# A feed-forward block in split fp32: weight sums stored by the first pass and loaded by the second, and low parts made by VectorE

## The chip, the cores and the metric

One core of a Trainium2 chip runs the whole program in one launch. The metric is the device time of one execution in microseconds (us). Below, TensorE is PE in the rows, VectorE is DVE, ScalarE is ACT, GpSimd is POOL, and SyncE, which here only issues transfers, is SP.

## What is computed

One layer of a hybrid transformer, over a prompt of 2048 tokens and a sample of 32 tokens: projections, two kinds of attention, an output projection, and a feed-forward block. Only the last matters here:

```python
def conv_ffn(h, conv_state, w_up, w_conv, b_conv, w_down):
    u = h @ w_up                                   # 1024 -> 2 x 2816
    padded = jnp.concatenate([conv_state, u], axis=1)
    uc = sum(padded[:, j:j + T] * w_conv[j] for j in range(CONV_W)) + b_conv
    a, g = jnp.split(uc, 2, axis=-1)
    return (jax.nn.silu(a) * g) @ w_down, padded[:, -(CONV_W - 1):]
```

The rest of the program, ahead of the block, is the same in both kernels.

## The kernel before, in words

**Split fp32.** Every factor x of a product is held as a high part (a copy in the type fp32r, made by ScalarE) and a low part (x minus the high part, made by VectorE or GpSimd). A product of two such factors is three matmuls: high by high, high by low, low by high (`three`, L2416 to L2423).

**Two passes over the up weights.** `w_up` is taken in 22 pairs of 128-column tiles: tile F (the half that goes through silu) and tile G. The 2080 tokens are five blocks of WT = 416. The first pass (wide, pairs 0 to 21) makes three blocks for each pair, the second (narrow, pairs 22 to 43, the same 22 weight tiles again) makes two. Two blocks at a time go through a Strassen scheme of seven products of half the depth, P1 to P7, four steps of depth each; the wide pass makes its third block in the plain way (SF and SG, eight steps each). So PE issues 7 x 4 x 3 = 84 matmuls of 416 columns for a narrow pair and 84 + 48 = 132 for a wide one. Its order is written out: P1, P5, P6, P2, (SF), P7, P3, P4, (SG) (`wide_pair`, `narrow_pair`, L2480 to L2499).

**What a pair needs.** P1, P2 and SF read the halves of tile F (`fwH`, `fwL` in the rows), P4 the second half of G and SG all of it, and P5, P6, P7, P3 read four sums of halves of F and G. VectorE makes the sums from the loaded tiles `fraw` (`sum_one` to `sum_four`, L2060 to L2077; `fsum_plain`, `fsL_plain`), ScalarE their high parts (`high_sum`, `fsH`), GpSimd their low parts (`low_sum`, L1608 to L1611, `fsL`). GpSimd also makes the low parts of both tiles (`low_half`, L1603 to L1606, `fwL`) and of some blocks of h2 (`low_block`, L1613 to L1615, `fright`). Both passes make the same sums.

**The other work of a pair.** The Strassen scheme chains through PSUM: ScalarE copies bank a to bank b (`seed_b`) and b to c (`seed_c`) between products, and takes bank e (`take_e`). VectorE takes two results (`take_c22`, which P4 of the same pair waits for, L2475 to L2478; `take_c12`), runs the three taps of the convolution over `fV` for F and for G (`taps`, L2095 to L2109), and multiplies silu(F) by G (`product`, L2137 to L2140). SyncE then stores the product to `act_d`. VectorE's slot of pair g is in this order: convolution G of pair g-1, product g-1, sums one and two of pair g+1, take c22, sum three, take c12, sum four, convolution F of pair g (`wide_slot`, `narrow_slot`, L2142 to L2161).

**Between the passes** the right-hand blocks are replaced: SyncE loads `late_blocks`, B11 and B21 (L1546 to L1552), VectorE makes T1 to T4 from them, ScalarE the high parts, VectorE and GpSimd the low parts (L2306 to L2338).

**Behind the second pass** `down(n)` multiplies 17 activation tiles by rows of `w_down` (66 matmuls of 512 columns for each tile and half); the 22 rows' low parts are shared by GpSimd (BY_POOL, L1677 to L1681) and VectorE (BY_DVE, `first_low`).

**Queues.** SyncE's queue runs in the order that it is written in: a wait at its head holds every later load and store. Of the second pass it is

```python
def next_up(g, i):
    sp.wait_ge(w_low[F], g + 1)
    sp.wait_ge(sums_ready, 4 * g + 4)
    load_up(i, F)
    sp.wait_ge(w_low[G], g + 1)
    load_up(i, G)
...
with sp.Fori(1, NF - 1) as i:
    next_up(NF + i, i + 1)
    store_narrow(i - 1)
```

## Time and profile before

| | |
|---|---|
| time, median of 3 runs | 3193.68 us (3192.21 to 3194.82) |
| time of the profiled execution | 3200.23 us |
| its span, first to last instruction | 3198.5 us |
| PE busy | 3009.9 us, 94% |
| VectorE busy | 1958.1 us, 61% |
| ScalarE busy | 1306.1 us, 41% |
| GpSimd busy | 1120.1 us, 35% |
| feed-forward up part | about 1649 to 2654 us of the span |
| data moved | 359.19 MB, mean 112 GB/s |

The profiled execution took 6.5 us more than the median of the runs. Times in the rows below are microseconds from the start of its span. A matmul's own time (0.35 us for 416 columns) overlaps the next one's, so the pace of PE is the count of matmuls over a stretch, not their durations.

### The profile page before, as it was taken

The page shows a single profiled execution, that of the slowest core. Times are in us where ns is not written, and L with a number is a line of the kernel's source. Part 1 is how long each engine was busy: PE and PEld are TensorE (multiplying, and loading weights), DVE is VectorE, ACT ScalarE, POOL GpSimd, SP SyncE. Part 2 cuts the span into 40 slices and gives each one's busy share as a digit, 9 for nine tenths or more (in the row PEclk, how much of TensorE's full clock was granted, in tenths as well). Part 3 has the DMA queues.
Part 4 walks back from the last instruction along what each step waited for, and adds up shares of the span by engine and source line. Part 5 has one row for each costly group of instructions (what it writes and reads, how often), then busy time and mean ns, then how long its engine had stood idle before and what let it go on. Part 6 is the DMA issues. An engine that isn't in the chain of part 4 may idle for free.

```text
span 3198.5 us, 48166 instructions
## 1 busy us (share of the span) xinstructions
PE 3009.9 (94%) x17216; PEld 2605.0 (81%) x17216; DVE 1958.1 (61%) x2517; ACT 1306.1 (41%) x2452; POOL 1120.1 (35%) x892
## 2 busy tenths in 40 slices
PE   7999998998999998999999999998899998999998
PEld 5788887776777887888879999998788886887886
DVE  2300035522998998675678787777999996224221
ACT  4611122213777887344554444444333333113110
POOL 3311012212666676120135444445555552002000
PEclk8999999998999999899999999999999999999999
DMA  6312224424422430885642222223222235434332
GB/s 216 112 65 77 73 82 143 134 96 115 126 56 55 90 69 16 274 275 186 217 144 73 68 65 68 67 68 97 70 80 81 79 97 185 166 125 162 124 126 71
DMA packets 299510, 359.19 MB, mean 112 GB/s; under 512 B 66204, under 2 KB 218456, under 8 KB 292572
## 3 DMA queue, kind: packets, MB, share of 16 engines
q1 hardware_dynamic: 283166, 307.83, 31.5%
q0 software_dynamic: 14864, 49.31, 4.5%
q8 instruction: 95, 1.56, 0.2%
q14 instruction: 53, 0.43, 0.0%
q10 hardware_dynamic: 1332, 0.06, 0.0%
HBM read 248.23 MB, written 108.89 MB: 112 GB/s over the span
## 4 chain that ended last, share of the span: by engine, by line
PE 40%; DVE 10%; issue 7%; DMA 2%; DVEq 1%; ACT 1%; POOL 0%; SPq 0%; ACTq 0%; POOLq 0%
PE facc L2422 16%; PE dacc L2528 14%; PE eacc L2401 6%; DVE fV L2099 2%; DVE fsum_plain L2063 1%; DVE fU L2126 1%; DVE fsL_plain L2072 1%; PE mpT L2548 1%; DVE fV L2103 1%; PE mpm L2558 1%; DVE fV L2108 1%; PE mpD L2539 0%; DMA w_out_plain<-w_out 0%; PE eyT L2384 0%; PE mpS L2568 0%
## 5 line engine op out<-in xcount | busy, mean ns | idle before, releaser
L2528 PE MATMUL dacc<-drows,dact 128*128 128x512 f32 (+1 forms) x2200 | 516.5, 397 | 16.4 <-DVE drows L2167 5.4
L2528 PEld LDWEIGHTS dacc<-drows,dact 128*128 128x128 f32 (+1 forms) x2200 | 412.6, 188 | 119.8 <-DVE drows L2167 6.2
L716 PE MATMUL pacc<-pring,h1H 128*128 128x512 f32 x1360 | 436.5, 398 | 8.8 <-POOL pring L584 5.5
L2422 PE MATMUL facc<-fright,fsH 128*128 128x416 f32 x1408 | 385.8, 355 | 18.0 <-ACT facc L1750 9.0
L1090 POOL TENSOR_TENSOR aS<-aS,aC 128x512 f32<-128x512 f32 (+3 forms) x326 | 334.6, 1034 | 166.8 <-DVE aC L1050 157.4
L1050 DVE TENSOR_TENSOR_SCAN aC<-aB,aC,a 128x512 f32<-128x512 f32 (+3 forms) x326 | 362.8, 1113 | 21.9 <-ACT aB L1008 10.6
L1605 POOL TENSOR_TENSOR fwL<-fraw,fwH 128x1024 fp32r<-128x1024 f32 x88 | 206.5, 2348 | 424.8 <-ACT fwH L1750 424.5
L2422 PE MATMUL facc<-fright,fwH 128*128 128x416 f32 x1056 | 302.2, 369 | 53.9 <-DVE fU L2087 49.2
L716 PEld LDWEIGHTS pacc<-pring,h1H 128*128 128x128 f32 x1360 | 259.6, 191 | 63.7 <-POOL pring L584 6.6
L2422 PEld LDWEIGHTS facc<-fright,fsH 128*128 128x128 f32 x1408 | 265.9, 191 | 24.8 <-issue 13.0
L2422 PEld LDWEIGHTS facc<-fright,fwH 128*128 128x128 f32 x1056 | 207.0, 198 | 65.0 <-issue 56.2
L716 PE MATMUL pacc<-pring,h1L 128*128 128x512 f32 x640 | 250.5, 393 | 0.0
L2422 PE MATMUL facc<-fright,fsL 128*128 128x416 f32 x704 | 250.2, 355 | 0.0
L2173 DVE TENSOR_TENSOR dact<-dact_plain,dact 128x2816 fp32r<-128x2816 f32 (+1 forms) x34 | 100.6, 2962 | 219.6 <-ACT dact L1750 219.6
L1750 ACT ACTIVATE dact<-dact_plain 128x2816 fp32r<-128x2816 f32 (+1 forms) x34 | 83.4, 2452 | 368.3 <-DMA dact_plain<-act_d 368.3
L1106 PE MATMUL a_z<-ak,aq 128*128 128x512 f32 (+3 forms) x640 | 209.7, 411 | 15.1 <-DMA aq<-qk_T 15.1
L1008 ACT ACTIVATE aB<-a_z 128x512 f32<-128x512 f32 (+3 forms) x326 | 180.1, 553 | 45.9 <-PE a_z L1117 21.0
L1132 PE MATMUL a_x<-ident,aS 128*128 128x128 f32 x1106 | 182.8, 282 | 10.2 <-ACT aA L1017 8.4
L2422 PE MATMUL facc<-fright,fwL 128*128 128x416 f32 x528 | 192.3, 364 | 0.0
L324 ACT ACTIVATE pstage<-pacc 128x512 f32<-128x512 f32 x112 | 66.6, 595 | 303.4 <-PE pacc L716 303.3
L2422 PE MATMUL facc<-fh,fwH 128*128 128x416 f32 x704 | 189.9, 351 | 0.0
L1626 POOL DMA_DIRECT2D y_out<-dy x34 | 18.4, 541 | 483.4 <-DVE dy L2190 483.4
(319 smaller groups left out, 6033.7 us busy)
## 6 DMA issues: line engine op xcount, KB each, us to landing
fraw<-w_up SPq DMA_DIRECT2D x88, 512.0 KB, 3.9
dact_plain<-act_d SPq DMA_DIRECT2D x32, 1408.0 KB, 6.4
proj_out<-pstage SPq DMA_DIRECT2D x119, 256.0 KB, 2.0
qk_T<-pturn POOLq DMA_DIRECT2D x68, 256.0 KB, 3.0
mwa<-w_ada SPq DMA_DIRECT2D x16, 1024.0 KB, 5.7
praw<-w_in SPq DMA_DIRECT2D x56, 256.0 KB, 2.8
aq<-qk_T SPq DMA_DIRECT2D x28, 512.0 KB, 12.0
mx<-proj_out SPq DMA_DIRECT2D x51, 256.0 KB, 5.0
```

Of the source, the lines that this page charges most:

```text
L716: op = mm_(acc[:, n % NB], h[:, kk, tok(t)], weight(q, w), start=(j == 0), stop=(j == len(order) - 1))
L1008: nc.scalar.activation(part(B, RB, n), part(Z, NZ, n), ACT.Sigmoid, scale=-1.0).then_inc(pass_ready, 1)
L1050: v.tensor_tensor_scan(buf[:, a:b][:, ::-1], part(B, RB, n)[:, ::-1], nought[:, 0:width(n)], buf[:, b:b + 1], ALU.mult, ALU.add).then_inc( ...
L1090: nc.gpsimd.tensor_tensor(at, at, buf[:, a + 1:b + 1], ALU.mult).then_inc(w_ready, 1)
L1106: mm = nc.tensor.matmul(to, Q[:, b, half, i * P:(i + 1) * P], K[:, b, span], start=(half == 0), stop=(half == 1), skip_group_check=True)
L1132: mm = nc.tensor.transpose(X[:, n % NX, j * P:(j + 1) * P], src[:, j * P:(j + 1) * P], c["ident"][:])
L1605: nc.gpsimd.tensor_tensor(upL[:, j, cols], raw[:, j, cols], upH[:, j, cols].bitcast(F32), ALU.subtract).then_inc(w_low[j], 1)
L1750: copy = lambda to, at: nc.scalar.activation(to, at, ACT.Copy)
L2173: v.tensor_tensor(to, acts_plain[n % 3][:, 1, :, 0:w], at[:, 0, :, 0:w].bitcast(F32), ALU.subtract).then_inc(a_low, 1)
L2401: mm = nc.tensor.matmul(acc[:, 1 - i.u, cols], a[:, i.u, kk], w[:, kk, cols], start=(kk == 0 and n == 0), stop=(kk == KD - 1 and n == len( ...
L2422: mm = nc.tensor.matmul(bank, a[:, kk], b[:, kk], start=(begins and kk == 0 and m == 0), stop=(kk == count - 1 and m == 2), skip_group_che ...
L2528: mm = nc.tensor.matmul(down_acc[0:rows, n % 2], at[:, l, kk, 0:rows], r, start=(kk == 0 and m == 0), stop=(kk == NF - 1 and m == len(pass ...
```

## The change

The four sums of a pair, high and low, stand side by side in one tile `fsums`. The first pass stores each split sum to HBM (`sums_d`, 4 x 512 KB for a pair); the second pass loads them instead of making them, and so needs only the second half of tile G. VectorE makes the low parts of tile F, of the sums and of the blocks; GpSimd keeps the low part of tile G. VectorE makes the low parts of all 22 rows of `w_down`. Slots of ScalarE, VectorE and SyncE are put in another order, and ScalarE's table for silu is loaded once ahead of the first pass. PE's order of products is the same; P5, P6, P7 and P3 of the second pass wait for loads.

```diff
+            def load_second(g, i):
+                sp.wait_ge(w_low[G], g + 1)
+                sp.dma_start(raw[:, G, KH:KD], d["w_up"].rearrange("(q p) n -> p q n", p=P)
+                             [:, KH:KD, bass.ds(FF + i * P, P)]).then_inc(raw_in[G], 16)
+            def store_sums(i):
+                own = bass.ds(i, 1)
+                for n in range(4):
+                    sp.wait_ge(s_low, 4 * i + n + 1)
+                    sp.dma_start(d["sums_d"][own, n].rearrange("o p e -> p (o e)"),
+                                 sums[:, n].bitcast(F32).rearrange("p a k e -> p (a k e)")).then_inc(sums_stored, 16)
+            def load_sum(n, g, i):
+                sp.wait_ge(done[("P5", "P6", "P7", "P3")[n]], g)
+                own = bass.ds(i, 1)
+                sp.dma_start(sums[:, n].bitcast(F32).rearrange("p a k e -> p (a k e)"),
+                             d["sums_d"][own, n].rearrange("o p e -> p (o e)")).then_inc(sums_in[n // 2], 16)
...
+            def narrow_loads(i):
+                sp.wait_ge(w_low[F], NF + i + 1)
+                load_up(i + 1, F)
+                load_second(NF + i, i + 1)
                 store_narrow(i - 1)
+                for n in range(4):
+                    load_sum(n, NF + i + 1, i + 1)
+            with sp.Fori(1, NF - 3) as i:
+                narrow_loads(i)
...
             def high_sum(n, g):
+                if n == 0:
+                    at_least(act, sums_stored, 64 * g)
...
                 seed_c(g)
+                high_sum(0, g + 1)
+                high_sum(1, g + 1)
                 take_c11(g, 2 + WT)
                 take_sf(g)
                 high_half(F, g + 1)
-                for n in range(4):
-                    high_sum(n, g + 1)
+                high_sum(2, g + 1)
+                high_sum(3, g + 1)
...
-            low_block(B11, b_first[0], 1)
-            low_sum(0, 0)
-            low_sum(1, 0)
-            low_block(B21, b_first[1], 2)
             store_h2(final)
-            low_sum(2, 0)
-            low_block(B22, b_first[2], 3)
-            low_sum(3, 0)
             with pool.Fori(1, NF) as i:
-                prepare(i, False)
...
+                low_half(G, i)
+            with pool.Fori(0, NF) as i:
+                low_half(G, NF + i, slice(KH, KD))
...
                 product(g - 1, WIDE)
                 sum_one(g + 1)
                 sum_two(g + 1)
+                low_sum(0, g + 1)
+                low_sum(1, g + 1)
+                low_half(F, g + 1)
                 take_c22(g, 2 + 2 * WT)
                 sum_three(g + 1)
+                low_sum(2, g + 1)
                 take_c12(g, 2 + 2 * WT)
                 sum_four(g + 1)
+                low_sum(3, g + 1)
                 conv_wide(g, g, F)
 
             def narrow_slot(g, i):
                 conv_narrow(g - 1, i - 1, G)
                 product(g - 1, NARROW)
-                sum_one(g + 1)
-                sum_two(g + 1)
+                low_half(F, g + 1)
                 take_c22(g, 2 + WT, True)
-                sum_three(g + 1)
                 take_c12(g, 2 + WT, True)
-                sum_four(g + 1)
                 conv_narrow(g, i, F)
...
+            def sums_are_in(n, g, wide):
+                if wide:
+                    pe.wait_ge(s_low, 4 * g + n + 1)
+                else:
+                    pe.wait_ge(sums_in[n // 2], 32 * (g - NF + 1))
```

The instructions of VectorE in the loop over narrow pairs, from the product of pair g-1 to the taking of c12, before:

```order
L2140 TENSOR_TENSOR fV<-fV 128x832
L2061 ISA
L44 ISA
L2063 TENSOR_TENSOR fsum_plain<-fraw 128x512
L2066 REGISTER_ALU
L44 REGISTER_ALU
L2068 TENSOR_TENSOR fsum_plain<-fsum_plain,fraw 128x512
L2087 TENSOR_TENSOR fU<-facc,fE 128x384
L2087 TENSOR_TENSOR fU<-facc,fE 128x32
L2072 TENSOR_TENSOR fsL_plain<-fraw 128x512
L2093 TENSOR_TENSOR fU<-facc,fE 128x384
L2093 TENSOR_TENSOR fU<-facc,fE 128x32
```

and now:

```order
L2178 TENSOR_TENSOR fV<-fV 128x832
L2084 REGISTER_ALU
L2085 TENSOR_TENSOR fwL<-fraw,fwH 128x1024
L2122 REGISTER_ALU
L2125 TENSOR_TENSOR fU<-facc,fE 128x384
L2125 TENSOR_TENSOR fU<-facc,fE 128x32
L2131 TENSOR_TENSOR fU<-facc,fE 128x384
L2131 TENSOR_TENSOR fU<-facc,fE 128x32
```

The sums (the fourth stands behind these rows, L2077) are gone; the low part of tile F has come in, ahead of the taking of c22.

SyncE's queue in the same loop, before (ISA rows are waits and set-up of the next transfer):

```order
L1441 DMA fraw<-w_up 128x8x128
L1441 ISA
L1441 DMA fraw<-w_up 128x8x128
L1465 ISA
L1465 DMA act_d<-fV 128x32
L1466 ISA
L1466 DMA act_d<-fV 128x6x128
L1468 ISA
L1468 DMA act_d<-fV 128x32
```

and now, of one of the pairs that are written out behind the loop:

```order
L1439 DMA fraw<-w_up 128x8x128
L1451 DMA fraw<-w_up 128x4x128
L1481 DMA act_d<-fV 128x32
L1482 DMA act_d<-fV 128x6x128
L1484 DMA act_d<-fV 128x32
L1464 DMA fsums<-sums_d 128x1024 x4
```

The second load of weights is half as large, and four loads of sums stand behind the three stores of the product.

SyncE's queue between the passes, before (`flate_blocks` are the late blocks, `fright_plain` are B11 and then B21):

```order
L1546 DMA flate_blocks<-h_d 128x8x416
L1441 DMA fraw<-w_up 128x8x128 x2
L1455 DMA act_d<-fV 128x9x128
L1457 DMA act_d<-fV 128x96
L1550 DMA fright_plain<-h_d 128x4x416
L1552 DMA fright_plain<-h_d 128x4x416
```

and now:

```order
L1565 DMA flate_blocks<-h_d 128x8x416
L1439 DMA fraw<-w_up 128x8x128
L1451 DMA fraw<-w_up 128x4x128
L1571 DMA fright_plain<-h_d 128x4x416
L1464 DMA fsums<-sums_d 128x1024 x2
L1471 DMA act_d<-fV 128x9x128
L1473 DMA act_d<-fV 128x96
L1577 DMA fright_plain<-h_d 128x4x416
```

B11's load stands ahead of the store of the product of pair 20, for which it had waited.

## Rows read from the trace of the kernel before

**Rows 1.** Busy time by stretch: the wide pass, then the narrow.
```profile
core 0: us, PE busy (x) PEld busy (x) DVE busy (x) ACT busy (x) POOL busy (x), PEclk, DMA share, GB/s
1721.00:2196.00 475.00, 475.00 (x2508) 468.24 (x2507) 374.52 (x286) 215.39 (x304) 220.70 (x114) 1.00 0.24 71
2264.00:2634.00 370.00, 336.86 (x1679) 325.63 (x1678) 361.36 (x581) 144.47 (x240) 204.22 (x120) 0.96 0.28 81
```

**Rows 2.** Timeline of PE, rows behind a gap: start, us, what, [idle before <-releaser].
```profile
1682.58 1.03 PE L2422 MATMUL facc<-fright,fsH 128*128 128x416 f32 x2 [3.92 <-issue]
...
2227.79 1.03 PE L2422 MATMUL facc<-fright,fwH 128*128 128x416 f32 x2 [12.50 <-DVE fU L2087]
...
2263.34 0.62 PE L2422 MATMUL facc<-fright,fwH 128*128 128x416 f32 x2 [3.52 <-DVE fU L2087]
...
2633.89 0.62 PE L2422 MATMUL facc<-fright,fwH 128*128 128x416 f32 x2 [0.79 <-DVE fU L2087]
2647.55 0.62 PE L2422 MATMUL facc<-fright,fsH 128*128 128x416 f32 x2 [2.02 <-ACT facc L1750]
2663.47 7.83 PE L2528 MATMUL dacc<-drows,dact 128*128 128x512 f32 x24 [5.04 <-DVE drows L2167]
...
2698.59 21.71 PE L2528 MATMUL dacc<-drows,dact 128*128 128x512 f32 x87 [4.09 <-DVE dy L2187]
```

**Rows 3.** VectorE's groups in 2281 to 2633 us: the four sums (busy, mean ns).
```profile
L2063 DVE TENSOR_TENSOR fsum_plain<-fraw 128x512 f32<-128x512 f32 x19 | 35.0, 1840 | 0.0
L2068 DVE TENSOR_TENSOR fsum_plain<-fsum_plain,fraw 128x512 f32<-128x512 f32 x20 | 33.1, 1654 | 2.5
...
L2072 DVE TENSOR_TENSOR fsL_plain<-fraw 128x512 f32<-128x512 f32 x19 | 23.5, 1236 | 0.0
L2077 DVE TENSOR_TENSOR fsL_plain<-fraw,fsum_plain 128x512 f32<-128x512 f32 x19 | 23.0, 1211 | 0.0
```

**Rows 4.** Timeline of VectorE: single instructions, GpSimd idle or waiting.
```profile
1629.23 1.23 DVE L2010 TENSOR_TENSOR emix<-emix,ex 128x1024 f32<-128x1024 f32 x1
1656.93 1.88 DVE L2276 TENSOR_TENSOR fright_plain<-fblocks,fright_plain 128x1664 f32<-128x1664 f32 x1
...
2001.30 0.92 DVE L2099 TENSOR_SCALAR fV<-fU,fcw,fcb 128x1248 f32<-128x1248 f32 x1
2002.37 1.52 DVE L2103 SCALAR_TENSOR_TENSOR fV<-fU,fcw,fV 128x1248 f32<-128x1248 f32 x1 [0.15 <-DVE fV L2099]
...
2007.04 0.69 DVE L2063 TENSOR_TENSOR fsum_plain<-fraw 128x512 f32<-128x512 f32 x1
```

**Rows 5.** Timelines of ScalarE, VectorE and PE in one wide pair.
```profile
1936.10 1.05 ACT L1750 ACTIVATE fwH<-fraw 128x1024 fp32r<-128x1024 f32 x1
1937.94 0.59 DVE L2087 TENSOR_TENSOR fU<-facc,fE 128x416 f32<-128x416 f32 x1 [4.44 <-PE facc L2422]
1940.00 0.55 PE L2422 MATMUL facc<-fright,fwH 128*128 128x416 f32 x2
```

**Rows 6.** Transfers: KB each, median us from issue to landing.
```profile
fraw<-w_up SPq DMA_DIRECT2D x36, 512.0 KB, 3.8
act_d<-fV SPq DMA_DIRECT2D x18, 384.0 KB, 2.8
...
dact_plain<-act_d SPq DMA_DIRECT2D x29, 1408.0 KB, 6.3
...
aq<-qk_T SPq DMA_DIRECT2D x28, 512.0 KB, 12.0
```

**Rows 7.** Timeline of VectorE between the passes.
```profile
2205.55 1.46 DVE L2140 TENSOR_TENSOR fV<-fV 128x1248 f32<-128x1248 f32 x1
2214.44 1.89 DVE L2312 TENSOR_TENSOR fright_plain<-flate_blocks,fright_plain 128x1664 f32<-128x1664 f32 x1 [7.43 <-DMA fright_plain<-h_d]
2216.43 5.42 DVE L2315 TENSOR_TENSOR fright_plain<-flate_blocks,fright_plain 128x1664 f32<-128x1664 f32 x1
```

**Rows 8.** The page's costliest groups: low parts of the activation tiles.
```profile
L2173 DVE TENSOR_TENSOR dact<-dact_plain,dact 128x2816 fp32r<-128x2816 f32 (+1 forms) x34 | 100.6, 2962 | 219.6 <-ACT dact L1750 219.6
```

More of the change, by code:

```diff
@@ L1228, in mlstm_output_ffn @@
     NARROW_STORES = 48
-    BY_DVE = (5, 7, 9, 11, 13, 15, *range(16, NF))
-    BY_POOL = tuple(kk for kk in range(NF) if kk not in BY_DVE)
     raw_in = [k.sem("w_up_f_loaded"), k.sem("w_up_g_loaded")]
@@ L1565, in _ @@
                 first_row(kk)
-            store_narrow(NF - 2)
+            for i in range(NF - 3, NF - 1):
+                narrow_loads(i)
             for kk in range(4, NF):
@@ L1768, in high_sum @@
                     at_least(act, done[("P5", "P6")[n]], g)
-                copy(sH[:, n], tmp[:, n] if n < 2 else sL_plain[:, n]).then_inc(s_high, 1)
+                copy(sums[:, n, 0], tmp[:, n] if n < 2 else sums_plain[:, n, 1]).then_inc(s_high, 1)
             def high_block(n, own):
@@ L1828, in wide_slot @@
                 high_half(F, g + 1)
-                for n in range(4):
-                    high_sum(n, g + 1)
+                high_sum(2, g + 1)
+                high_sum(3, g + 1)
                 take_c21(g, 2 + WT)
@@ L1841, in narrow_slot @@
                 high_half(F, g + 1, True)
-                for n in range(4):
-                    high_sum(n, g + 1)
                 take_c21(g, 2)
@@ L1935, in _ @@
             high_half(G, NF, True)
-            narrow_slot(NF, WIDE)
-            with act.Fori(1, NF - 1) as i:
+            g = NF
+            seed_b(g, False)
+            silu(g - 1, WIDE)
+            take_e(g)
+            seed_c(g)
+            take_c11(g, 2)
+            high_half(F, g + 1, True)
+            take_c21(g, 2)
+            high_half(G, g + 1, True)
+            with act.Fori(1, NF - 2) as i:
                 narrow_slot(NF + i, NARROW)
-            g = 2 * NF - 1
+            g = 2 * NF - 2
             seed_b(g, False)
@@ L1944, in _ @@
             seed_c(g)
+            take_c11(g, 2)
+            high_half(F, g + 1, True)
             for kk in range(4):
                 first_high(kk)
+            take_c21(g, 2)
+            high_half(G, g + 1, True)
+            g = 2 * NF - 1
+            seed_b(g, False)
+            silu(g - 1, NARROW)
+            take_e(g)
+            seed_c(g)
+            for kk in range(4, 7):
+                first_high(kk)
             take_c11(g, 2)
-            for kk in range(4, 16):
+            for kk in range(7, 13):
                 first_high(kk)
             take_c21(g, 2)
+            for kk in range(13, 16):
+                first_high(kk)
             silu(g, NARROW)
@@ L2329, in _ @@
             conv_wide(g, g, F)
+            low_block(B21, plain(B21), 5)
             low_t(T3, 7, 7)
+            low_block(B22, late_blocks[:, KH:KD], 6)
             conv_wide(g, g, G)
-            product(g, WIDE)
+            dve.wait_ge(conv_done, 2 * NF)
+            g = NF
+            take_c22(g, 2 + WT, True)
             low_t(T4, 8, 8)
-            g = NF
-            sum_one(g + 1)
-            sum_two(g + 1)
+            low_half(F, g + 1)
+            product(g - 1, WIDE)
+            take_c12(g, 2 + WT, True)
+            conv_narrow(g, 0, F)
+            with dve.Fori(1, NF - 2) as i:
+                narrow_slot(NF + i, i)
+            g = 2 * NF - 2
+            conv_narrow(g - 1, NF - 3, G)
+            product(g - 1, NARROW)
+            act_low(0)
+            low_half(F, g + 1)
             take_c22(g, 2 + WT, True)
-            sum_three(g + 1)
             take_c12(g, 2 + WT, True)
-            sum_four(g + 1)
-            conv_narrow(g, 0, F)
-            with dve.Fori(1, NF - 1) as i:
-                narrow_slot(NF + i, i)
+            for kk in range(4):
+                first_low(kk)
+            conv_narrow(g, NF - 2, F)
             g = 2 * NF - 1
@@ L2346, in _ @@
             product(g - 1, NARROW)
-            act_low(0)
+            for kk in range(4, 7):
+                first_low(kk)
             take_c22(g, 2 + WT, True)
+            for kk in range(7, 10):
+                first_low(kk)
             take_c12(g, 2 + WT, True)
             conv_narrow(g, NF - 1, F)
-            for kk in BY_DVE[:4]:
+            for kk in range(10, 13):
                 first_low(kk)
             conv_narrow(g, NF - 1, G)
-            for kk in BY_DVE[4:]:
+            for kk in range(13, 16):
+                first_low(kk)
+            product(g, NARROW)
+            for kk in range(16, NF):
                 first_low(kk)
             act_low(1)
-            product(g, NARROW)
             dve.wait_ge(act_stored, (WIDE_STORES + NARROW_STORES) * NF)
```

198 lines of the change are left out of this document (101 added, 97 removed).

## The prediction, made blind

> **What bounds the kernel now.** I read the busy time by stretch first. In the wide pass [rows 1] PE is busy for all of 475 us, in which it begins 2508 matmuls: one each 0.1894 us, so 132 of them, a wide pair, take 25.0 us. Nothing that only lightens another engine can shorten that stretch. In the narrow pass PE is busy for 336.9 of 370 us, its granted clock is 0.96 of full speed, and VectorE is busy for 361.4, which is 98% of it. At the pace of the wide pass 84 matmuls take 15.9 us. The timeline of PE [rows 2] gives what they do take: P4 of pair 22 begins at 2263.3, that of pair 42 at 2633.9, so 20 pairs have 18.53 us each. The reader is to see that the gap inside a pair always stands before P4 (`fwH` with `fright` there), and that its releaser is VectorE's L2087, the taking of c22. VectorE is the bound of the narrow pass, and PE waits for it once a pair. The four sums cost VectorE (35.0 + 33.1 + 23.5 + 23.0)/19 = 6.03 us a pair [rows 3], though a 512-wide one alone takes 0.69 us [rows 4]: they run while GpSimd makes low parts.
>
> Then the seams [rows 2]: 12.5 us of gap before P4 of pair 21, 35.55 us from there to P4 of pair 22 (2227.79 to 2263.34), 5.04 us in the first down tile, 4.09 us before the third.
>
> **The narrow pairs.** VectorE now spends 361.4/20 = 18.07 us a pair. The change takes 6.03 away and adds one 1024-wide low part at 1.23 [rows 4]: 13.3 us, without counting that what is left is held up less. That is below PE's 15.9. ScalarE loses four high parts and GpSimd all but one instruction, neither was near its limit [rows 1]. P4's wait: the low part of F needs its high part, which waits for P2 (9.1 us into the pair by 4 x 12 matmuls) and takes 1.05 [rows 5]; with the take of c11 ahead of it (0.5, an estimate from the 0.59 of the same width, rows 5) that is 10.7; low part 11.9, c22 12.6; P4 is due at 6 x 12 x 0.1894 = 13.6. Margin 1 us. I therefore take 15.9 us a pair. P4 of pair 43 begins now 2.02 + 15.9 us behind that of pair 42, at 2651.8. From P4 of pair 22 that is 388.5 us for 21 pairs; 21 x 15.91 = 334.1, and 0.5 for the first pair, in which VectorE is late: **-54 us**. The clock comes with it: it is 1.00 in the pass without gaps and 0.96 in this one [rows 1], and 15.91 is the pace at 1.00.
>
> **The loads of sums.** They are new in each narrow pair: 4 x 512 KB, less 256 KB of weights. No row shows this load. From below: one 1408 KB load of long rows takes 6.3 us [rows 6], so the 1024 KB that P5 waits for (its semaphore counts sums one and two) some 5. From above: the 512 KB load of `aq` took 12.0 in another stage. The loads stand on SyncE behind the store of the product of the pair before. So there is a loop over two pairs: from P5 of pair g-1 five products to P3's end (11.4), c12 (0.6), convolutions F and G and the product (18.07 - 6.03 - 2 x 0.6 = 10.8), stores at most 2.8 [rows 6], the second issue 0.6 (an estimate from the spacing of such issues, bounded by the 2.8), then a load of L: twice the period is 26.2 + L, against 31.8. At L = 5 the loads are in time, by 0.6 us; a 3.8 [rows 6] gives more, the 12.0 less: 19.1 us a pair. I take 5, since the sums' rows of 4 KB are nearest to the 1408 KB load.
>
> **Between the passes.** P4 of pair 21 was due at 2227.79 - 12.50 = 2215.3. VectorE had finished product 20 at 2207.0 and sat idle 7.43 us for B11 [rows 7], whose load stood behind that product's store. Now the load goes ahead of it, as soon as P1 of the pair is done and the weights are asked for, some 6 us earlier, so it lands about when the product ends. Then T1, low B11, T2, low T1 at 1.88 [rows 4] and c22: 2207.0 + 4 x 1.88 + 0.6 = 2215.1. The gap goes: **-12 us**. The second subtraction took 5.42 [rows 7] where it ran beside GpSimd's low block, and 1.88 without [rows 4]; if such times stay, 3.5 us of the 12 do not come.
>
> The Trainium skill's SBUF — State Buffer (section SBUF: two separate sides) says that a VectorE operation with two inputs in SBUF and a GpSimd operation that reads SBUF hold a shared port by turns, for whole instructions. By that rule the sum takes the 1.88, because no GpSimd instruction is left here but one; without it, it would be -9.
>
> From P4 of pair 21 to P4 of pair 22 VectorE has low F 1.23, c12 and c22 1.2, seven 1664-wide operations 13.2, two convolutions of 0.92 + 1.52 + 1.52 + 0.3 of waits [rows 4], 8.5: 24.1 us, and with 1.6 for waits on ScalarE 25.7, where 35.55 stood; PE alone needs 108 matmuls, 20.5. **-9.8 us**, at best -15, at worst nothing.
>
> **The wide pairs.** VectorE gets four low sums (4 x 0.69) and low F (1.23): 4.0 us on top of 374.5/19 = 19.7 in a pair of 25.0, still below PE even if nothing gets shorter. What is on the path is the low part of F, now ahead of c22: the high part ends at 1937.15 [rows 5], low part 1938.4, c22 1939.0, P4 at 1940.0. One us to spare, so nothing, up to +1 for each of 21 pairs. ScalarE's first high sum waits until the four sums of the pair before have been stored. The last is split some 22 us into the pair before and is needed 10 us into this one; the 384 KB store takes 2.8 [rows 6]. Twelve us of cover; if it is gone, ScalarE stops ahead of c11 and high F, and P1 of the next pair with it. I take nothing.
>
> **Start.** P7 of pair 0 begins at 1682.58 [rows 2]. Its chain is reordered: GpSimd's low blocks go to VectorE, but a table load and three more copies now stand ahead of `seed_c`. Either sign: I take -2, with -5 and +3 as ends.
>
> **End.** The low parts of the 22 rows are all VectorE's, spread over the last two pairs. Behind P4 of pair 43 it still has twelve at 0.69, one convolution and a product (5.5, a half of the 10.8 above) and act_low(1) at 2.96 [rows 8]: with what is left of convolution F some 18.5 us, while the first down tile needs 66 matmuls, about 15.7 (an estimate from the width, 512/416 x 0.1894 x 66 = 15.4). So 3 us of gap in place of 5.04 + 4.09 [rows 2], and the 2.02 before P7 counted above; with less time at the lower clock behind gaps **-8 us**, between -11 and 0.
>
> **Sum**: -54 - 12 - 9.8 - 2 - 8 = -85.8, against the profiled execution 3200.2 - 85.8 = 3114.4. The median of the runs is 6.5 us below that execution, so I predict 3108.
>
> **Rivals.**
>
> *The loads set the pace, still faster.* L is near the 12.0: 19.1 us a pair would give back 21 x 3.2 = 67 us, 3175; L = 8, the middle, 17.1 us a pair: 3133. For it: the loads run beside a load of weights and a store, the core moves 71 to 81 GB/s now and would move some 200. Against: the cover of 0.6 us at L = 5 is reckoned with VectorE's slow times.
>
> *The loads set the pace and the kernel is slower.* The same loop from L = 13.8 on: the period is then 20.0, 4.1 us over 15.9, and 21 x 4.1 = 86 eats the whole sum. If the two loads of 512 KB come one behind the other at 12.0 each, L = 24 and the period 25.1: +193 - 86 = +107, 3301. Against: a 1408 KB load takes 6.3.
>
> In a sentence of its own: the Trainium skill's DMA: Bandwidth & Descriptors (Latency and other measured facts) gives an HBM access 0.2 us on average and 2 us at high load. By that rule L would be about 2 us longer than the 5, 7 us: that is 16.6 us a pair, 14 us of the sum, 3122, and it speaks against this change; no row here shows a load of sums.
>
> *VectorE stays late.* The margins of 1 us before P4 are less than the true hold-ups in both passes. If the narrow pairs keep half of their stalls (1.3 of 2.6 us) and the wide ones get 0.5: +27 +10, 3145.
>
> *No gain.* The 6.03 come off VectorE but P4's wait was set by something else on the same engine order; then only the seams gain: 3162. If these don't either, 3194.
>
> **Chances.** Forecast with its bounds, 3090 to 3125: 0.62. Loads set the pace, faster: 0.15. VectorE late: 0.12. Only seams: 0.04. Nothing: 0.02. Slower: 0.05. Best case (every seam at its lower bound: -15, -11, -5 for -9.8, -8, -2) is 11 below, 3097, and 3088 takes in the rest of the profiled execution's 6.5. The range goes from 3088 to 3150, which leaves out the upper part of the loads' case, the last three cases and little more. A difference of 0.2% (6.4 us) is about what a measurement can tell from none. Faster by more 0.93, within 0.02, slower 0.05.
>
> **What would show it.** In the changed profile: PE busy for the whole of the narrow pass, clock 1.00, P4 to P4 in 15.9 us; VectorE below 14 us a pair; no gap before P4 of pair 21; the wide pass still 25.0 a pair. Wrong: gaps before P5 (`fsums`, released by a DMA) say that the loads set the pace; gaps before P4 released by `fU` that VectorE is late; gaps before P1 or SF in the wide pass that the stores hold ScalarE.

## The result, and the profile after

The changed kernel takes 3111.44 us (median of 4 runs, 3110.65 to 3118.24), the kernel before 3192.94 us beside it (4 runs, 3191.77 to 3194.82): ratio 0.9749, 95% interval 0.9732 to 0.9766, 81.5 us less. Forecast were 3108.0 and a range of 3088 to 3150. The profiled execution of the changed kernel took 3110.72 us, its span is 3109.0.

Busy time by stretch, of the changed kernel: the wide pass, then the narrow, with the columns of [rows 1].

```profile
1721.00:2190.00 469.00, 469.00 (x2478) 464.33 (x2477) 352.90 (x378) 166.34 (x261) 44.85 (x18) 1.00 0.45 153
2240.00:2560.00 320.00, 317.79 (x1671) 313.16 (x1671) 240.56 (x528) 102.33 (x164) 25.65 (x20) 1.00 0.66 215
```

The wide pass begins a matmul every 469.00/2478 = 0.1893 us, as before [rows 1]. In the narrow pass PE is now busy for 317.8 of 320 us at a granted clock of 1.00, where it had 0.96, and VectorE for 75% of the time instead of 98%. The transfers have gone from 0.28 to 0.66 of their engines' time.

The timeline of PE, rows behind a gap, answers to [rows 2]. The first four are the start, the next three the seam between the passes and the first narrow pairs, the last three the narrow pass's end and the first down tile.

```profile
1656.67 0.65 PE L2488 MATMUL facc<-fright,fwH 128*128 128x416 f32 x2 [1.82 <-DVE fright L2094]
...
1664.73 3.43 PE L2488 MATMUL facc<-fright,fsums 128*128 128x416 f32 x12 [2.45 <-DVE fsums L2090]
...
1677.09 7.50 PE L2488 MATMUL facc<-fright,fsums 128*128 128x416 f32 x24 [6.02 <-ACT facc L1754]
...
1707.99 0.62 PE L2488 MATMUL facc<-fright,fwH 128*128 128x416 f32 x2 [2.19 <-DVE fU L2125]
...
2209.27 0.62 PE L2488 MATMUL facc<-fright,fwH 128*128 128x416 f32 x2 [1.04 <-DVE fU L2125]
...
2233.86 0.64 PE L2488 MATMUL facc<-fright,fwH 128*128 128x416 f32 x2 [3.02 <-DVE fright L2081]
...
2256.34 3.85 PE L2488 MATMUL facc<-fright,fsums 128*128 128x416 f32 x19 [1.24 <-DMA fsums<-sums_d]
...
2539.95 0.61 PE L2488 MATMUL facc<-fright,fwH 128*128 128x416 f32 x2 [0.89 <-DVE fU L2125]
...
2583.20 3.40 PE L2597 MATMUL dacc<-drows,dact 128*128 128x512 f32 x9 [1.85 <-DVE drows L2207]
...
2588.57 9.21 PE L2597 MATMUL dacc<-drows,dact 128*128 128x512 f32 x27 [1.97 <-DVE drows L2207]
```

P4 of pair 21 (2209.27) waits 1.04 us where it waited 12.50, P4 of pair 22 stands at 2233.86, and from there to 2539.95 there is one gap, of 1.24 us, before P5 of pair 24: it waits for the first sums that SyncE's loop loads (those of pairs 22 and 23 are loaded ahead of it). VectorE and GpSimd in one narrow pair (timeline of the changed kernel):

```profile
2328.83 1.23 DVE L2085 TENSOR_TENSOR fwL<-fraw,fwH 128x1024 fp32r<-128x1024 f32 x1 [2.38 <-ACT fwH L1754]
2329.97 0.65 DVE L2125 TENSOR_TENSOR fU<-facc,fE 128x384 f32<-128x384 f32 x2
...
2335.19 1.29 POOL L1645 TENSOR_TENSOR fwL<-fraw,fwH 128x512 fp32r<-128x512 f32 x1 [14.64 <-ACT fwH L1754]
2335.32 2.19 DVE L2146 SCALAR_TENSOR_TENSOR fV<-fU,fcw,fV 128x800 f32<-128x800 f32 x2
...
2344.78 1.23 DVE L2085 TENSOR_TENSOR fwL<-fraw,fwH 128x1024 fp32r<-128x1024 f32 x1 [2.39 <-ACT fwH L1754]
```

The pattern repeats after 2344.78 - 2328.83 = 15.95 us, PE's own pace, and VectorE sits idle 2.4 us ahead of each low part: it now waits for work. The transfers of the changed kernel (the page's part 6):

```profile
sums_d<-fsums SPq DMA_DIRECT2D x88, 512.0 KB, 2.9
fsums<-sums_d SPq DMA_DIRECT2D x88, 512.0 KB, 4.7
```

### The profile page after: what moved, and what is told of

The parts are those of the page before. It is cut to its first block, busy times and chain, and to the rows that moved or that the text cites. A ratio compares the mean times of both kernels' runs of the same rounds, so it can differ in the third digit from the quotient of the medians.

```text
span 3109.0 us, 48048 instructions
## 1 busy us (share of the span) xinstructions
PE 2977.4 (96%) x17216; PEld 2586.1 (83%) x17216; DVE 1787.9 (58%) x2576; ACT 1207.5 (39%) x2325; POOL 676.5 (22%) x657
## 4 chain that ended last, share of the span: by engine, by line
PE 35%; issue 18%; DVE 3%; DMA 2%; SPq 0%; ACT 0%; POOL 0%; POOLq 0%; DVEq 0%; ACTq 0%
PE dacc L2597 15%; PE facc L2488 9%; PE eacc L2467 6%; PE mpm L2627 1%; PE mpT L2617 1%; DMA w_out_plain<-w_out 1%; PE eyT L2450 0%; PE mpN L2653 0%; PE mpN L2657 0%; PE mpD L2608 0%; PE mpS L2637 0%; PE mpT L2668 0%; PE exT L2480 0%; DMA dring<-w_down 0%; DMA fraw<-w_up 0%
## 5 line engine op out<-in xcount | busy, mean ns | idle before, releaser
L2488 PE MATMUL facc<-fright,fsums 128*128 128x416 f32 x2112 | 418.0, 354 | 10.8 <-ACT facc L1754 6.5
L2488 PEld LDWEIGHTS facc<-fright,fsums 128*128 128x128 f32 x2112 | 398.2, 190 | 16.7 <-issue 9.0
L2488 PE MATMUL facc<-fright,fwH 128*128 128x416 f32 x1056 | 288.5, 354 | 9.6 <-DVE fU L2125 4.1
L1645 POOL TENSOR_TENSOR fwL<-fraw,fwH 128x1024 fp32r<-128x1024 f32 (+1 forms) x45 | 88.0, 1959 | 810.3 <-ACT fwH L1754 810.3
L2488 PEld LDWEIGHTS facc<-fright,fwH 128*128 128x128 f32 x1056 | 198.7, 189 | 14.5 <-issue 5.5
L2488 PE MATMUL facc<-fright,fwL 128*128 128x416 f32 x528 | 185.8, 352 | 0.0
L716 PE MATMUL pacc<-plate,h1H 128*128 128x512 f32 x544 | 180.3, 397 | 5.3 <-POOL plate L584 5.3
L1013 ACT ACTIVATE aS<-a_z 128x512 f32<-128x512 f32 (+3 forms) x326 | 182.3, 559 | 0.0
```

The costliest lines, as they stand in the source:

```text
L716: op = mm_(acc[:, n % NB], h[:, kk, tok(t)], weight(q, w), start=(j == 0), stop=(j == len(order) - 1))
L1013: nc.scalar.activation(part(S, RS, n), part(Z, NZ, n), ACT.Sigmoid).then_inc(stop_ready, 1)
L1645: nc.gpsimd.tensor_tensor(upL[:, j, cols], raw[:, j, cols], upH[:, j, cols].bitcast(F32), ALU.subtract).then_inc(w_low[j], 1)
L2488: mm = nc.tensor.matmul(bank, a[:, kk], b[:, kk], start=(begins and kk == 0 and m == 0), stop=(kk == count - 1 and m == 2), skip_group_che ...
```

## The experiments

Eleven kernels ran, in three groups, each group on one chip beside the kernel before (3194.21, 3194.08 and 3192.86 us there). The code ahead of the feed-forward block is the same in all, yet P1 of pair 0 begins between 1653.7 and 1663.8 in the profiled executions. So next to the medians stands the time from that P1 to the end of the span. It leaves out P1's own wait, 3.6 us in the kernel before and 1.8 in the changed one. The changed kernel itself did not run in the first two groups, so a difference from it there is between groups; the ratios, each against the kernel before of its own group, are the safer measure.

| kernel | median, us | ratio to before, 95% | P1(0) to end | P4 to P4, narrow |
|---|---|---|---|---|
| before | 3192.9 | 1 | 1535.0 | 18.53 |
| changed, first time | 3111.4 | 0.9732 to 0.9766 | 1452.3 | 15.95 |
| after_again | 3110.9 | 0.9726 to 0.9753 | 1453.9 | 15.95 |
| no_loads | 3108.6 | 0.9720 to 0.9747 | 1451.4 | 15.95 |
| made_again | 3197.4 | 1.0002 to 1.0020 | 1537.4 | 19.50 |
| loads_only | 3107.4 | 0.9714 to 0.9741 | 1448.4 | 15.95 |
| made_by_pool | 3178.3 | 0.9939 to 0.9967 | 1518.8 | 18.55 |
| twice | 3125.9 | 0.9766 to 0.9793 | 1462.7 | 16.14 |
| b11_first | 3188.7 | 0.9974 to 0.9992 | 1527.8 | |
| start | 3111.2 | 0.9724 to 0.9750 | 1450.4 | |
| tail | 3109.9 | 0.9718 to 0.9745 | 1448.2 | |
| three | 3104.9 | 0.9709 to 0.9735 | 1447.9 | |
| best | 3104.0 | 0.9708 to 0.9736 | 1448.8 | |

The theory was that the narrow pass gained because VectorE is rid of making sums, with the loads hidden. The first rival was that the low parts' move off GpSimd did it, by ending its contention with VectorE; the second that the loads are near the pace.

### Sums loaded or made, low parts by VectorE or GpSimd

Four kernels make a square: the changed one, `loads_only`, `made_again` and `made_by_pool`.

`made_again`, against the changed kernel (ScalarE's high parts of the sums, SyncE's loads of whole G tiles and PE's waits for `s_low` go back with it):

```diff
             def narrow_slot(g, i):
                 product(g - 1, NARROW)
+                sum_one(g + 1)
+                sum_two(g + 1)
+                low_sum(0, g + 1)
+                low_sum(1, g + 1)
                 low_half(F, g + 1)
                 take_c22(g, 2 + WT, True)
+                sum_three(g + 1)
+                low_sum(2, g + 1)
                 take_c12(g, 2 + WT, True)
+                sum_four(g + 1)
+                low_sum(3, g + 1)
...
-                store_sums(i + 1)
...
-                for n in range(4):
-                    load_sum(n, NF + i + 1, i + 1)
```

> The second pass makes the four sums again (VectorE the sums, ScalarE the high parts, VectorE the low parts); nothing of them is stored or loaded, and the low parts are still VectorE's. Theory (taking the 6 us of sums off VectorE is what the narrow pass gained by; without it VectorE has 12.0 + 8 x 0.69 = 17.5 us a pair, and late waits for ScalarE's high parts besides): P4 to P4 16.9 to 18.5 us, so 20 to 54 us more than the changed kernel, 3131 to 3165. Rival (moving the low parts off GpSimd is what helped, since VectorE's own operations became shorter): within 5 us of the changed kernel, P4 to P4 16.0.

Measured 3197.4 us, 86 above the changed kernel and by 0.1% slower than the kernel before. The theory had the direction and too small a size, the rival is refuted. P4 to P4 takes 19.50 us. Two neighbouring gaps of PE in `made_again`:

```profile
2300.56 0.80 PE L2507 MATMUL facc<-fright,fwH 128*128 128x416 f32 x2 [3.32 <-DVE fU L2112]
...
2320.01 0.62 PE L2507 MATMUL facc<-fright,fwH 128*128 128x416 f32 x2 [1.73 <-DVE fU L2112]
```

VectorE's groups over 17 pairs of it (busy, mean ns, idle before), and below them the same two sums in `made_by_pool`:

```profile
L2078 DVE TENSOR_TENSOR fsums<-fsums_plain,fsums 128x512 fp32r<-128x512 f32 x34 | 23.6, 693 | 23.7 <-ACT fsums L1739 23.7
...
L2073 DVE TENSOR_TENSOR fwL<-fraw,fwH 128x1024 fp32r<-128x1024 f32 x17 | 20.8, 1225 | 11.2 <-ACT fwH L1739 11.2
...
L2097 DVE TENSOR_TENSOR fsums_plain<-fraw 128x512 f32<-128x512 f32 x18 | 12.3, 682 | 0.0
...
L2102 DVE TENSOR_TENSOR fsums_plain<-fraw,fsum_plain 128x512 f32<-128x512 f32 x17 | 11.6, 682 | 0.0
```

```profile
L2116 DVE TENSOR_TENSOR fsums_plain<-fraw,fsum_plain 128x512 f32<-128x512 f32 x18 | 30.8, 1709 | 0.0
L2111 DVE TENSOR_TENSOR fsums_plain<-fraw 128x512 f32<-128x512 f32 x17 | 25.9, 1522 | 0.0
```

VectorE alone makes each sum in 0.68 us, where [rows 3] had 1.2 to 1.8. So contention was real. But the work that it then has itself, four low sums at 0.69 and the low part of F at 1.23, brings it to 16.9 us a pair (busy 287.06 us over 17 pairs), and it stands idle for another 2.6, most of it (23.7 + 11.2 us in 17 pairs) for a high part that ScalarE makes just ahead. The expectation named these waits, but its upper end of 18.5 us left too little for them.

`made_by_pool` gives those low parts to GpSimd again:

> The sums made again in the second pass, as in made_again, and the low parts of tile F and of the sums made by GpSimd inside the loops, as in loads_only: the fourth corner of the square, with the seams of the change. Theory (with sums to make VectorE sets the narrow pace whoever makes the low parts, and GpSimd's low parts cost it less than its own would, by the 2.4 us a pair that it idles for high parts in made_again): P4 to P4 18.3 to 18.8 us as in the kernel before, 50 to 62 us more than the changed kernel. Rival (the order of the change's slots, not who makes the low parts, costs made_again its 19.5): P4 to P4 19.3 or more, 75 us or more above the changed kernel.

Measured 3178.3 us, 67.5 above `after_again` in its group, P4 to P4 18.55: the theory's pace, with 5.5 us more in total than its upper end. VectorE is busy for 307.28 of 320 us there. The loop gaps now stand before P1 and are released by GpSimd's low part of F, so that VectorE alone sets the pace isn't shown. Beside the kernel before it is 14.5 us faster with the same pace of narrow pairs: that is what the reordered seams are worth, net, without any load of sums. Of the change's gain between P4 of pair 21 and P4 of pair 22, from 35.55 to 24.59 us, 6.4 us are here too (29.16); the other 4.6 go only with the loads.

`loads_only` keeps the loads and gives GpSimd the loops' low parts:

```diff
+            low_half(G, 1)
+            with pool.Fori(2, NF) as i:
+                low_sum(0, i)
+                low_sum(1, i)
+                low_half(F, i)
+                low_sum(2, i)
+                low_sum(3, i)
                 low_half(G, i)
...
+            with pool.Fori(2, NF) as i:
+                low_half(F, NF + i)
                 low_half(G, NF + i, slice(KH, KD))
...
             def narrow_slot(g, i):
                 product(g - 1, NARROW)
-                low_half(F, g + 1)
```

> Sums are stored and loaded as in the change, but inside the loops the low parts of tile F and of the sums are GpSimd's again. Theory (the loads carry the gain, PE is the bound of both passes whoever makes the low parts): narrow pass 15.9 to 16.2 us from P4 to P4, wide pass 25.0, 0 to 6 us more than the changed kernel. Rival (contention between GpSimd and VectorE was what held the narrow pass): 20 us or more above the changed kernel, gaps before P4 released by the taking of c22.

Measured 3107.4 us: not slower than the changed kernel, if anything faster (the intervals overlap). Its stretch of fifteen narrow pairs, and below it that of the changed kernel:

```profile
2280.00:2520.00 240.00, 240.00 (x1266) 237.08 (x1265) 161.39 (x376) 73.87 (x120) 56.18 (x31) 1.00 0.64 208
```

```profile
2280.00:2520.00 240.00, 240.00 (x1266) 237.39 (x1265) 177.23 (x390) 74.69 (x122) 19.43 (x15) 1.00 0.64 207
```

The same 1266 matmuls in 240 us, with no gap. Loading the sums is worth 2.6 us a pair with the low parts on GpSimd and 3.55 with them on VectorE; handing the loops' low parts to VectorE is worth nothing beside the loads and costs 0.95 us a pair without them. This settles the first rival: it fell. The contention was real and is gone, but in `loads_only` it goes with the sums themselves, without the move.

### The loads

> Leaves out the loads of sums: the second pass uses, for all of its 22 pairs, the split sums of pair 21 that stand in the tile (another result). Theory (the loads are hidden behind the products, their only price is the 1.24 us of gap before the first P5 of the pass): 1 to 3 us less than the changed kernel, P4 to P4 still 15.9 us. Rival (the loads are near the pace, or slow other engines through contention): 8 us or more less, and P4 to P4 shorter than 15.94.

It leaves the loads out: `load_sum` is empty and PE waits for `4 * NF` low sums instead. Measured 3108.6 us, 2.3 to 2.9 less than the two measurements of the changed kernel, with intervals that overlap; from P1(0) to the end 0.9 to 2.5 less, and P4 to P4 the same 15.95. These are the theory's numbers: the loads slow nothing in the steady pairs. The expectation calls the 1.24 us a gap before the first P5 of the pass; it is the third, that of pair 24.

In `twice` a copy of equal size goes with each load in the loop:

```diff
                 for n in range(4):
                     load_sum(n, NF + i + 1, i + 1)
+                    sp.dma_start(d["sums_x"][bass.ds(i + 1, 1), n], d["sums_d"][bass.ds(i + 1, 1), n]).then_inc(copied, 16)
```

> Beside each of the loads of sums of 18 narrow pairs stands a copy of the same 512 KB from HBM to HBM, which doubles the bytes that are read for sums and adds as many written ones. Theory (the transfers are hidden but not by far: DMA share 0.66 now, the loop over two pairs had about 1 us to spare at a load of 5 us for two sums): the loads get late, gaps before P5 released by the load of sums, P4 to P4 16.5 to 19 us, 10 to 55 us more than the changed kernel. Rival (the loads have wide cover): within 3 us of it, no gap before P5.

Measured 3125.9 us, 14.5 to 15.1 above the changed kernel: inside the theory's total, but for the larger part by another mechanism. The stretch of narrow pairs in `twice`, then rows of PE's and ScalarE's timelines, and SyncE's (start, us, transfer issued):

```profile
2280.00:2520.00 240.00, 238.39 (x1250) 233.38 (x1249) 174.96 (x389) 74.06 (x119) 18.21 (x15) 1.00 0.96 331
```

```profile
2263.72 4.80 PE L2491 MATMUL facc<-fright,fsums 128*128 128x416 f32 x24 [2.55 <-DMA fsums<-sums_d]
...
2296.76 4.81 PE L2491 MATMUL facc<-fright,fsums 128*128 128x416 f32 x24 [0.90 <-DMA fsums<-sums_d]
...
2555.08 1.03 PE L2491 MATMUL facc<-fright,fwH 128*128 128x416 f32 x2 [5.42 <-DVE fU L2128]
```

```profile
2545.24 0.52 ACT L1757 ACTIVATE fU<-facc 128x416 f32<-128x416 f32 x1 [1.88 <-PE facc L2491]
...
2552.05 1.06 ACT L1757 ACTIVATE fwH<-fraw 128x1024 fp32r<-128x1024 f32 x1 [6.29 <-DMA fraw<-w_up]
```

```profile
2538.52 0.45 SPq L1440 DMA_DIRECT2D fraw<-w_up  x1
2539.01 7.55 SPq L1452 DMA_DIRECT2D fraw<-w_up  x1
```

With the DMA engines busy for 0.96 of the time a load of a sum lands after 6.8 us instead of 4.7. PE idles for 1.6 of 240 us and begins 1250 matmuls for 1266, 3.0 us of work less. The cover can be read at P5, as medians over pairs 25 to 41. In the changed kernel the second of its two sums lands 5.5 us after the first was issued, 2.1 us ahead of P5 (never less than 1.3). In `twice` it takes 7.7 us and lands 0.2 ahead, and in 8 of these 17 pairs P5 begins 0.12 us behind the landing, as it also does where it has waited. So the cover is some 2 us and is used up here. Neither side had it right: it is not wide, as the rival had it, and the pace goes only to 16.14, less than the theory's 16.5.

From P4 of pair 22 to that of pair 43 `twice` takes 12.0 us longer than the changed kernel. 3.0 of them lie in pairs 24 to 40, 2.2 in the two pairs ahead (the gap of 2.55 is in them, 1.24 in the changed kernel), and 6.7 in two pairs behind, where activation and down weights join the traffic: an issue is held 7.55 us, the weights of tile F come 6.29 us late, and P4 waits 5.42. What costs the most time is not the sums but the next pair's weights behind them.

### The seam between the passes

`b11_first` is the kernel before with one edit:

```diff
             next_up(NF - 1, 0)
-            store_wide(NF - 2)
             sp.wait_ge(done["P1"], NF)
             sp.dma_start(plain(B11), d["h2_d"][:, 0:KH, WIDE:WIDE + WT]).then_inc(h_in, 16)
+            store_wide(NF - 2)
```

> The kernel before with one edit of the change alone: the load of B11 stands ahead of the store of product 20 in SyncE's queue. Theory (of the 12.5 us of gap before P4 of pair 21, the 7.4 that VectorE sat idle for B11 come from that place in the queue, and the rest from the sums and the slow second subtraction beside GpSimd's low block): gap 5 to 8 us, 4 to 8 us less than the kernel before. Rival (B11 is held by the load of weights or by P1, not by the store): gap 11 us or more, no change.

Measured 3188.7 us, 5.3 less than the kernel before, within the theory's 4 to 8. PE's gap and VectorE's second subtraction there, and GpSimd at that place in the kernel before:

```profile
2213.25 1.03 PE L2422 MATMUL facc<-fright,fwH 128*128 128x416 f32 x2 [6.05 <-DVE fU L2087]
```

```profile
2201.79 5.52 DVE L2315 TENSOR_TENSOR fright_plain<-flate_blocks,fright_plain 128x1664 f32<-128x1664 f32 x1
```

```profile
2216.41 3.70 POOL L1615 TENSOR_TENSOR fright<-fright_plain,fright 128x1664 fp32r<-128x1664 f32 x1 [14.94 <-DVE fright_plain L2312]
```

Half of the 12.5 us was the place in the queue. The other half goes only with the rest of the change: the second subtraction still takes 5.52 us. It began at 2216.43 in [rows 7], just behind GpSimd's low block (2216.41, 3.70 us), and ended 1.74 us after that block did. In the changed kernel, where GpSimd is idle:

```profile
2201.13 1.89 DVE L2365 TENSOR_TENSOR fright_plain<-flate_blocks,fright_plain 128x1664 f32<-128x1664 f32 x1 [2.65 <-DMA fright_plain<-h_d]
...
2202.93 1.89 DVE L2094 TENSOR_TENSOR fright<-fright_plain,fright 128x1664 fp32r<-128x1664 f32 x1
...
2204.74 1.89 DVE L2369 TENSOR_TENSOR fright_plain<-flate_blocks,fright_plain 128x1664 f32<-128x1664 f32 x1
```

### Versions that might beat both kernels

`start` moves `seed_c(0)` ahead of `high_t(T3, 4)` on ScalarE; `tail` moves `store_narrow(NF - 2)` from row 7 to row 16; `three` has both and the low part of the late B22 on GpSimd; `best` has both and the loops of `loads_only`.

```diff
             seed_b(0, True)
+            seed_c(0)
             high_t(T3, 4)
...
-            seed_c(0)
...
-                if kk == 7:
+                if kk == 16:
                     store_narrow(NF - 2)
```

> The changed kernel with the first copy of bank b to bank c (seed_c of pair 0) ahead of ScalarE's high part of T3, no longer behind the table load. Theory (P7 of pair 0 waits 6.0 us for that copy): gap before P7 0 to 3 us, 3 to 6 us less than the changed kernel. Rival (P7 then waits for the low part of T3 or of sum three instead): less than 1.5 us.

Measured 3111.2 us, no gain that the runs resolve. The gap before P7 of pair 0 falls from 6.02 to 2.71 us as the theory said, and what then ends it is the low part of T3, as the rival said. P6 of pair 1 waits 3.60 us in its place, for the copy to bank b, which stands on ScalarE behind the high sums of pair 1; their first was held until the sums of pair 0 had been stored. From P1(0) to P4(1) it is 48.7 us instead of 51.3. Two gaps of PE in `start`, then ScalarE's row:

```profile
1676.98 4.91 PE L2488 MATMUL facc<-fright,fsums 128*128 128x416 f32 x24 [2.71 <-DVE fright L2081]
...
1692.62 4.03 PE L2488 MATMUL facc<-fright,fsums 128*128 128x416 f32 x12 [3.60 <-ACT facc L1754]
```

```profile
1684.60 1.15 ACT L1754 ACTIVATE fsums<-fsum_plain 128x512 fp32r<-128x512 f32 x2 [2.66 <-DMA sums_d<-fsums]
```

> The changed kernel with the store of product 42 behind the load of row 16 of the down weights, not ahead of row 7. Theory (that store waits for the product and holds the loads of rows, so ScalarE and VectorE sit idle for rows 7 us each, and PE waits 1.85 + 1.97 us in the first down tile): 2 to 4 us less than the changed kernel. Rival (the activation tiles or PE's pace set the end): within 1 us.

The median, 3109.9 us, says 1 to 1.5 less; the profiled execution, with P1(0) late at 1663.8, has 4.1 less from P1(0) to the end. The gaps from the first down matmul to the second tile's fall only from 3.82 to 3.45 us, but the granted clock stays up. The 20 us from the first down matmul on, in the changed kernel, in `start` and in `tail`:

```profile
2574.19:2594.19 20.00, 16.18 (x53) 12.11 (x53) 17.42 (x39) 12.04 (x18) 0.00 (x0) 0.75 0.76 266
```

```profile
2574.26:2594.26 20.00, 15.31 (x64) 11.47 (x63) 17.98 (x39) 11.95 (x18) 0.00 (x0) 1.00 0.77 275
```

```profile
2580.62:2600.62 20.00, 16.55 (x70) 12.55 (x70) 17.90 (x32) 8.66 (x12) 0.00 (x0) 1.00 0.68 217
```

In the changed kernel the clock is at 0.50 (1.2 GHz) for about half of these 20 us and PE begins 53 matmuls; in `tail` it is at 1.00 and PE begins 70. From the first tile's start to the second's it is 23.6 and 19.8 us, and the clock is the larger part of the difference between these two. It isn't what the edit is worth: in `start`, which does not have the edit, the clock stays at 1.00 too, with gaps of 6.0 us in total, and the tile takes 22.6. Over all kernels with the changed narrow pass the tile takes 22.6 to 23.6 us without the edit (six profiles) and 18.3 to 19.8 with it (`tail`, `three`, `best`). So the edit brings 2.8 us or more there; how the time without it divides between gaps and lower clock changes from one execution to the next.

> The changed kernel with both edits (first copy to bank c early, store of product 42 later), and the low part of the late block B22 made by GpSimd instead of VectorE. Theory (the 3.0 us before P4 of pair 22 come from VectorE's list, from which 1.9 us are taken): 6 to 12 us less than the changed kernel, gap before P4 of pair 22 about 1 us. Rival (GpSimd's low part slows VectorE beside it by as much as it takes off): what the two other edits give, 5 to 9 us.

Measured 3104.9 us, 6.0 to 6.6 less: the lower end of the theory. But its own mechanism failed. The gap before P4 of pair 22 is 3.92 us, not 1. GpSimd and VectorE in `three`:

```profile
2222.26 1.89 DVE L2085 TENSOR_TENSOR fright<-fright_plain,fright 128x1664 fp32r<-128x1664 f32 x1
2222.49 5.29 POOL L1687 TENSOR_TENSOR fright<-flate_blocks,fright 128x1664 fp32r<-128x1664 f32 x1 [4.82 <-DVE fright L2098]
...
2224.06 3.74 DVE L2162 COPY fhist<-fU 128x2 f32<-128x2 f32 x1
```

A copy of two elements, 0.17 us beside an idle GpSimd, takes 3.74 us and ends with GpSimd's instruction (both at 2227.8): the 1.9 us taken off VectorE came back as a wait twice as long.

> loads_only with the edits of start and tail: the sums loaded, the loops' low parts by GpSimd, the first copy to bank c early, the store of product 42 late. Theory (the three gains lie in different places and add: 4, 2 and 4 us from the start of P1 of pair 0 to the end): 7 to 11 us less than the changed kernel, 3100 to 3104. Rival (they share the same waits): no more than 4 us less.

Measured 3104.0 us, 6.8 less than `after_again` by the medians; the means of the five runs of each differ by 5.3, give or take 3.9 (95%). It beats both kernels, but the gains did not add: from P1(0) to the end 1448.8, no less than `loads_only` alone. Its profile says where they went. Behind P4 of pair 43 it is 3.6 us shorter than `loads_only`, about what `tail` has against the changed kernel (3.5); the start is no shorter, 49.0 us from P1(0) to P4(1) in both, so the edit of the start gave nothing here; and from P4 of pair 21 to P4 of pair 24 it takes 62.5 us for 58.7. In these pairs stands a wait of 2.10 us for the first sums that the loop loads, which `loads_only` has at 0.3 and the changed kernel at 1.24. That wait differs between executions of one kernel: `after_again`, the changed kernel once more, has 0.18, because PE came late to it. Behind the gap of 3.02 us that both have before P4 of pair 22, 6 us of the changed kernel and of `after_again`:

```profile
2234.00:2240.00 6.00, 6.00 (x32) 5.95 (x33) 3.02 (x6) 1.54 (x3) 1.29 (x1) 1.00 0.54 156
```

```profile
2234.00:2240.00 6.00, 6.00 (x22) 5.74 (x21) 1.94 (x5) 1.03 (x2) 1.29 (x1) 0.60 0.54 157
```

Whether the 3.7 us come from the edits or from the execution isn't shown.

> The changed kernel as it is, beside the next two on one chip. Both theories: 3107 to 3113 us; it is the mark for the others of this group.

Measured 3110.9 us, as expected.

## Why the prediction was right

By its own steps, between the two profiled executions (3200.2 and 3110.7):

| step | forecast | measured | by |
|---|---|---|---|
| narrow pairs, P4(22) to P4(43) | -54 | -50.8 | [rows 2]; 2233.86 + 338.1 |
| gap before P4(21) | -12 | -11.5 | 12.50 to 1.04 |
| P4(21) to P4(22) | -9.8 | -11.0 | 35.55 to 24.59 |
| wide pairs | 0 | 0 | 0.1893 us a matmul |
| start | -2 | -2.0 | the block's first matmul to P4(21), less its gap; -0.4 of it up to P7(0) |
| end, behind P4(43) | -8 | -9.2 | 546.3 to 537.1 |
| sum | -85.8 | -84.4 | before rounding |

The start's term was argued for P7 of pair 0, where only -0.4 came; 1.4 more came by P4 of pair 1, so its size is luck. The rest of the 89.5 us, 5.1, lies ahead of the block in code that did not change: the profiled execution of before took 6.5 us more than the median, which the forecast had allowed for.

**Narrow pairs.** The pace is 15.95 us (forecast 15.91) and VectorE has 240.56/20.07 = 12.0 us a pair (forecast 13.3). The missing 3.2 us are, nearly all, the wait for the loop's first sums (1.24), a late pair (0.89) and 0.04 in each of 21 pairs (0.8). The reason given holds too: loading the sums brings 2.6 to 3.55 us a pair. One share was misread. The 6.03 us of sums in [rows 3] are 2.7 us of work (4 x 0.68) and 3.3 of contention with GpSimd's low sums; I took them for one cost. It made no difference, since loading them also takes the low sums off GpSimd, and it is why the move of F's low part to VectorE was not needed.

**Loads.** For L, the time from the first issue until two sums have landed, I took 5 us, and a cover of 0.6. A sum lands 4.7 us after its issue (median), the second is issued 0.8 after the first, and L is 5.5, longer than taken. The cover is longer as well. SyncE and PE in the changed kernel:

```profile
2344.43 3.77 SPq L1464 DMA_DIRECT2D fsums<-sums_d  x4
```

```profile
2352.09 4.15 PE L2488 MATMUL facc<-fright,fsums 128*128 128x416 f32 x21
```

In this pair the second sum lands at 2350.67 and P5 begins at 2352.09: 1.4 us to spare, and 2.1 in the median pair. The cover came out longer because the rest of the loop was taken too long: VectorE is 1.3 us a pair faster than I reckoned, and the stores are issued, not landed, when the loads go out. So that the loads stay hidden was right, with two errors of opposite sign in its sum. The two rivals on the loads had .20 between them, and the experiment `twice` shows how near they were: at L = 7.7 the cover is gone. Their price was too high, though: the forecast's loop gives (26.2 + 7.7)/2 = 17.0 us a pair there, and 16.14 were measured.

The Trainium skill's DMA: Bandwidth & Descriptors (Latency and other measured facts) gives an HBM access 2 us at high load, from which the prediction had estimated L at 7 us. This case's trace has 5.5 at the change's own DMA share of 0.64 to 0.66, and 7.7 only at a share of 0.96.

**Between the passes.** B11 landed 2.65 us behind the product's end, not with it; c22 was taken by 2209.1 with P4 due at 2208.2, hence 1.04 of gap; the other profiles of kernels with loaded sums have 0.00 to 0.66 there. The second subtraction took 1.89 us, the value chosen, and not 5.42.

The Trainium skill's SBUF — State Buffer (SBUF: two separate sides) has the two engines hold the shared port by turns for whole instructions. The subtraction that ended 1.74 us behind GpSimd's block, about its own length, agrees, and so do both sides of `three`: GpSimd's block, begun 0.23 us behind a subtraction of VectorE, took 5.29 us for 3.70, and the copy then ended with it. The copy has one input, so which of the rule's cases holds for it can't be told from these rows. Such copies were long before the change too: from 1700 to 2600 us their median is 1.03 us in the kernel before and 0.17 in the changed one.

**Wide pairs.** No gap from 1721 to 2190: the margin of 1 us and the stores' cover held. Only at the start, in pair 1, where the sums of pair 0 are made late, do the stores hold ScalarE, as `start` showed.

**End.** Right in size, wrong in cause: luck. The forecast took it from the gaps of 5.04 and 4.09 us. The second is gone. The first became 1.85 + 1.97, so the first two tiles together, that gap included, are 5.1 us shorter. The other 4.1 us were not forecast: 1.7 in the third tile, behind the gap that is gone, and 2.4 later, around a wait of 1.71 us for GpSimd's rows that this profile of the changed kernel lacks and `after_again` has at 0.82. None of it needs the loads: `made_again` has 537.7 us behind P4(43). For the first tile I had VectorE late with a long list; in the trace ScalarE and VectorE stand idle for rows, 7.76 and 5.66 us. ScalarE's row in the changed kernel:

```profile
2575.84 1.68 ACT L1754 ACTIVATE drows<-drows_plain 128x512 fp32r<-128x512 f32 x3 [7.76 <-DMA drows_plain<-w_down]
```

The loads of rows 7 and up stand behind the store of product 42, which waits for the product. `tail` moves that store and the tile gets 2.8 us or more shorter, so the place in the queue was a part of the wait that the forecast did not have.

## What to carry to other kernels

When PE waits once an iteration for one overloaded engine, the work worth removing is what that engine repeats from an earlier pass. Storing it costs transfers that can hide behind a loop with slack, and the check is the loop over two iterations, store to load to use, not the bandwidth alone; here it left 2 us. Before moving work between VectorE and GpSimd, split each slow row into its duration alone and its hold-up by the other engine, and count the waits of a high-part, low-part chain between engines: here the move alone cost 0.95 us a pair. And compare versions from a common event in the block, since code ahead of it can shift by more than the edit is worth.
